# Attention on one core: two thirds of a pair's scores move between the products of the pair in front, and the halves of the outputs move behind the next pair's first softmax step

## What is computed

```python
q = (hn @ w_q).reshape(bsz, seq_len, N_KV_HEADS, GQ, HEAD_DIM)
...
s = jnp.einsum('bnqkgd,bnskd->bnkgqs', q, k) * (HEAD_DIM ** -0.5)
s = s + bias[None]                       # ALiBi, banded by chunks of 64 frames
sk = sink[None, None, :, :, None, None]
m = jnp.maximum(jnp.max(s, axis=-1, keepdims=True), sk)
p = jnp.exp(s - m)
p = p / (jnp.sum(p, axis=-1, keepdims=True) + jnp.exp(sk - m))
o = jnp.einsum('bnkgqs,bnskd->bnqkgd', p, v)
...
return jnp.concatenate([o_meta, o_real], axis=1) @ w_o
```

## Time and profile before

| what | us |
|---|---|
| three runs, median (lowest to highest) | 1196.5 (1194.91 to 1196.95) |
| the profiled execution: its own time | 1193.38 |
| span of its records | 1191.6 |
| TensorE busy in the span | 1114.3 (94%) |
| VectorE, ScalarE, GpSimd busy | 495.5, 486.4, 639.2 |
| stretch 651 to 757 of the span (the eight pairs): TensorE busy | 94.26 of 106.00 |
| mean granted TensorE clock | 0.969 |

### The profile page before, as it was taken

How to read it: one execution, slowest core, us unless ns; L and a number is a source line. 1 busy time by engine, 2 the same in 40 slices (tenths; PEclk the granted TensorE clock), 3 DMA queues, 4 the chain that set the end, 5 groups by cost and what they waited for, 6 DMA issues and landing times.

```text
span 1191.6 us, 28327 instructions
## 1 busy us (share of the span) xinstructions
PE 1114.3 (94%) x10546; PEld 1091.9 (92%) x10546; DVE 495.5 (42%) x853; ACT 486.4 (41%) x880; POOL 639.2 (54%) x540
## 2 busy tenths in 40 slices
PE   4576899999999999999999989899999999999996
PEld 3465799999999999999999888899999999999996
DVE  6988121254444444311115766435444444421111
ACT  5843243444444444322324544445444444432222
POOL 4993065555555555664544454665555555565451
PEclk7589899999999999999999999999999999999998
DMA  7055533333333333332323333233333333333321
GB/s 151 17 138 136 144 107 89 88 87 91 88 88 88 88 88 93 106 98 87 94 71 84 99 82 82 72 88 90 96 89 96 88 88 97 98 109 87 96 62 71
DMA packets 218326, 110.51 MB, mean 93 GB/s; under 512 B 33207, under 2 KB 215367, under 8 KB 217943
## 3 DMA queue, kind: packets, MB, share of 16 engines
q1 hardware_dynamic: 212327, 105.68, 31.9%
q10 hardware_dynamic: 5938, 3.99, 1.1%
HBM read 103.31 MB, written 6.32 MB: 92 GB/s over the span
## 4 chain that ended last, share of the span: by engine, by line
PE 82%; DVE 4%; DMA 3%; issue 3%; ACT 3%; POOL 2%; SPq 1%; ACTq 1%; POOLq 0%; DVEq 0%
PE slot L1199 77%; DMA brow<-in_s_b_im 1%; POOL w_lo L1916 1%; PE slot L1120 1%; POOL prob L2030 1%; PE slot L1114 1%; DMA xt<-in_x 1%; PE slot L1083 1%; ACT prob L961 1%; PE slot L1067 1%; PE slot L1097 0%; DMA v_scratch<-vtok 0%; ACT x_raw L736 0%; DMA kern_scratch<-kern 0%; ACTq L463 0%
## 5 line engine op out<-in xcount | busy, mean ns | idle before, releaser
L1916 POOL TENSOR_TENSOR w_lo<-raw,w_hi 128x512 fp32r<-128x512 f32 (+2 forms) x312 | 430.0, 1381 | 433.5 <-ACT w_hi L624 418.4
L624 ACT ACTIVATE w_hi<-raw 128x512 fp32r<-128x512 f32 (+2 forms) x308 | 202.5, 662 | 395.8 <-PE slot L1199 392.0
L1199 PE MATMUL slot<-xa_hi,w_hi 128*128 128x264 f32 (+1 forms) x1472 | 298.6, 284 | 0.9 <-DVE xa_lo L1678 0.9
L1199 PE MATMUL slot<-xa_hi,w_lo 128*128 128x264 f32 (+1 forms) x1472 | 298.4, 284 | 0.0
L1199 PE MATMUL slot<-xa_lo,w_hi 128*128 128x264 f32 (+1 forms) x1472 | 298.1, 284 | 0.0
L1199 PEld LDWEIGHTS slot<-xa_hi,w_hi 128*128 128x128 f32 x1472 | 229.0, 189 | 1.3 <-issue 1.1
L1199 PEld LDWEIGHTS slot<-xa_lo,w_hi 128*128 128x128 f32 x1472 | 228.3, 189 | 0.0
L1199 PEld LDWEIGHTS slot<-xa_hi,w_lo 128*128 128x128 f32 x1472 | 227.8, 189 | 0.0
L1199 PE MATMUL slot<-act_hi,w_hi 128*128 128x264 f32 (+1 forms) x704 | 141.8, 282 | 0.0
L1199 PE MATMUL slot<-act_lo,w_hi 128*128 128x264 f32 (+1 forms) x704 | 141.6, 282 | 0.0
L1199 PE MATMUL slot<-act_hi,w_lo 128*128 128x264 f32 (+1 forms) x704 | 141.2, 282 | 0.0
(11 more groups left out here) (285 smaller groups left out, 1481.0 us busy)
## 6 DMA issues: line engine op xcount, KB each, us to landing
raw<-in_ffn_w_up SPq DMA_DIRECT2D x176, 256.0 KB, 2.9
raw<-in_ffn_w_down SPq DMA_DIRECT2D x32, 384.0 KB, 3.3
raw<-in_ffn_w_down SPq DMA_DIRECT2D x32, 320.0 KB, 3.0
raw<-in_s_w_glu SPq DMA_DIRECT2D x32, 256.0 KB, 2.8
toep<-kern_scratch SPq DMA_DIRECT2D x64, 64.0 KB, 2.6
raw<-in_w_q SPq DMA_DIRECT2D x16, 256.0 KB, 3.3
raw<-in_w_o SPq DMA_DIRECT2D x16, 256.0 KB, 2.8
gelu_scratch<-x_raw ACTq DMA_DIRECT2D x8, 264.0 KB, 2.5
```

Of the source, the lines that this page charges most:

```text
L624: run(buffer_of(w_hi_all, buf, nk), buffer_of(raw_all, buf, nk), ACT.Copy).then_inc(hi_done, 1)
L1199: ins = mm(slot[dst][:, half, 0:b - a], w, xx[:, k, a:b], start=k == 0 and n == 0, stop=k == nk - 1 and n == 2)
L1916: tt(buffer_of(w_lo_all, buf, nk), buffer_of(raw_all, buf, nk), f32(buffer_of(w_hi_all, buf, nk)), ALU.subtract).then_inc(lo_done, 1)
```

## The change

Three pieces of work are put at other places; none is added or removed.

- TensorE: the scores of a pair's groups 0 and 1 (`first_scores`, 12 of 18 matmuls) are issued in the pair in front of it, behind that pair's product of group 0, and those of group 2 (`last_scores`) behind its product of group 2. The waits for the queries (`q_evicted`), for K (`k_in`) and for the copies out of the banks of groups 0 and 1 stand before the third block of the product of group 0; the first two stood before the product of group 2.
- ScalarE: the high half of a pair's output (`high_half`) is copied in the next pair, behind the exponentials of its group 0.
- VectorE: the low half (`low_half`) is written in the next pair, behind `scores(2)`, before the denominators of group 1.

In the last pair, the slab of the output projection no longer waits at its start for all seven outputs, but before each k tile for that one (`out_ready`).

The two halves that belong to the last pair stand behind it, as before.

```diff
@@ -950,6 +950,11 @@
                     slot[2][:, :, :].rearrange("p a (n c) -> p a n c", n=4), ACT.Copy).then_inc(v_copied, 1)
                 run(vtok[0:META, 4, :], slot[3][0:META, 0, 0:2 * P], ACT.Copy).then_inc(v_copied, 1)
 
+                def high_half(hp):
+                    act.wait_ge(pv_done, hp + 1)
+                    run(tile_of(ao_hi, hp, META, L), slot[2][:, 1, :], ACT.Copy)
+                    run(tile_of(ao_hi, hp, 0, META), slot[3][:, 0, 0:META], ACT.Copy).then_inc(ao_hi_done, 1)
+
                 def heads(j, hp, par):
 
                     for t in range(GRP):
@@ -961,11 +966,14 @@
                             ins = run(prob[:, par, n, :], prob[:, par, n, :], ACT.Exp, bias=mneg[:, par, n:n + 1],
                                       accum_out=den[:, par, n:n + 1])
                         ins.then_inc(exp_done, 1)
+                        if t == 0:
+
+                            if not isinstance(hp, int):
+                                high_half(act.snap(hp - 1))
+                            elif hp >= 1:
+                                high_half(hp - 1)
                     for n in range(2):
                         split_at(S_Q, j, 4 + 2 * par + n, KC)
-                    act.wait_ge(pv_done, hp + 1)
-                    run(tile_of(ao_hi, hp, META, L), slot[2][:, 1, :], ACT.Copy)
-                    run(tile_of(ao_hi, hp, 0, META), slot[3][:, 0, 0:META], ACT.Copy).then_inc(ao_hi_done, 1)
 
                 heads(0, 0, 0)
                 heads(0, 1, 1)
@@ -974,6 +982,7 @@
                         heads(j, act.snap(j * 2 + e), e)
                 heads(KVH - 1, HP - 2, 0)
                 heads(KVH - 1, HP - 1, 1)
+                high_half(HP - 1)
 
 
                 def o_tile(j, m, par):
@@ -1332,30 +1341,35 @@
                 bank = [slot[1][:, 0, :], slot[1][:, 1, :], slot[2][:, 0, :]]
                 o_real, o_meta = slot[2][:, 1, :], slot[3][:, 0, :]
 
+                def score(e, t, n):
+                    for x in range(2):
+                        part, rows = (slice(h * CH, (h + 1) * CH) for h in (x, x ^ SWAP[t]))
+                        ins = mm(bank[t][rows, n * KEYS:(n + 1) * KEYS], qt[part, e, GRP * t + n, :],
+                                 kcur[part, GRP * t + n, :], start=True, stop=True)
+                    if n == GRP - 1:
+                        ins.then_inc(scores_done, 1)
+
+                def first_scores(e):
+
+                    for n in range(GRP):
+                        score(e, 0, n)
+                        score(e, 1, n)
+
+                def last_scores(e):
+                    for n in range(GRP):
+                        score(e, 2, n)
+
+                def out_ready(k):
+                    pe.wait_ge(ao_hi_done, k + 1)
+                    pe.wait_ge(ao_lo_done, k + 1)
+
                 def heads(j, hp, e, ahead):
                     peeled = isinstance(hp, int)
-                    def score(t, n):
-                        for x in range(2):
-                            part, rows = (slice(h * CH, (h + 1) * CH) for h in (x, x ^ SWAP[t]))
-                            ins = mm(bank[t][rows, n * KEYS:(n + 1) * KEYS], qt[part, e, GRP * t + n, :],
-                                     kcur[part, GRP * t + n, :], start=True, stop=True)
-                        if n == GRP - 1:
-                            ins.then_inc(scores_done, 1)
-
-
-                    for n in range(GRP):
-                        score(0, n)
-                        score(1, n)
-                    for n in range(GRP):
-                        score(2, n)
                     if ahead:
                         q_slab(hp + 1, 1 - e, part=(0, Q_PART))
-
                     else:
                         pe.wait_ge(q_evicted, HP)
-                        pe.wait_ge(ao_hi_done, HP - 1)
-                        pe.wait_ge(ao_lo_done, HP - 1)
-                        slab(S_O, (KC, KC), 0, 0, ao_hi, ao_lo, tokens=LIVE_TOKENS, part=(0, HP - 1))
+                        slab(S_O, (KC, KC), 0, 0, ao_hi, ao_lo, ready=out_ready, tokens=LIVE_TOKENS, part=(0, HP - 1))
 
                     def transposes(t):
                         pe.wait_ge(p_ready, hp * GRP + (t + 1))
@@ -1364,11 +1378,18 @@
                         tr(bank[t][0:GRP * META, GRP * P:(GRP + 1) * P], probm[:, e, GRP * t:GRP * (t + 1), :].rearrange("p n j -> p (n j)"),
                            ident[:, :]).then_inc(pt_full, 1)
 
-                    def product(t):
+                    def product(t, scores_next=False):
 
                         pe.wait_ge(pt_copied, hp * GRP + (t + 1))
                         for n in range(GRP):
                             blk = GRP * t + n
+                            if scores_next and n == GRP - 1:
+
+
+                                pe.wait_ge(q_evicted, hp + 2)
+                                if e == 1:
+                                    pe.wait_ge(k_in, j * 96 + 192)
+                                pe.wait_ge(pt_copied, hp * GRP + 2)
                             for half in range(2):
                                 part = slice(half * HD, (half + 1) * HD)
                                 src = slice((half ^ SWAP[t]) * HD, ((half ^ SWAP[t]) + 1) * HD)
@@ -1387,17 +1408,18 @@
                     if not peeled or hp >= 1:
                         pe.wait_ge(ao_lo_done, hp)
                     pe.wait_ge(v_in, j * 80 + 80)
-                    product(0)
+                    product(0, ahead)
+                    if ahead:
+                        first_scores(1 - e)
                     product(1)
+                    product(2).then_inc(pv_done, 1)
                     if ahead:
-                        pe.wait_ge(q_evicted, hp + 2)
-                        if e == 1:
-                            pe.wait_ge(k_in, j * 96 + 192)
-
-                    product(2).then_inc(pv_done, 1)
+                        last_scores(1 - e)
 
                 pe.wait_ge(q_evicted, 1)
                 pe.wait_ge(k_in, 96)
+                first_scores(0)
+                last_scores(0)
                 heads(0, 0, 0, True)
                 heads(0, 1, 1, True)
                 with pe.Fori(1, KVH - 1) as j:
@@ -1781,6 +1803,11 @@
                     scores(1)
                     denominators(0)
                     scores(2)
+
+                    if not isinstance(hp, int):
+                        low_half(dve.snap(hp - 1))
+                    elif hp >= 1:
+                        low_half(hp - 1)
                     denominators(1)
                     denominators(2)
                     for t in range(GRP):
@@ -1793,6 +1820,7 @@
                         copy(pt[:, three, :], bank[t][:, 0:GRP * P].rearrange("p (n q) -> p n q", n=GRP))
                         copy(ptm[0:GRP * META, t, :], bank[t][0:GRP * META, GRP * P:(GRP + 1) * P]
                              ).then_inc(pt_copied, 1)
+                def low_half(hp):
                     dve.wait_ge(ao_hi_done, hp + 1)
                     tt(tile_of(ao_lo, hp, META, L), slot[2][:, 1, :], f32(tile_of(ao_hi, hp, META, L)), ALU.subtract)
                     tt(tile_of(ao_lo, hp, 0, META), slot[3][:, 0, 0:META], f32(tile_of(ao_hi, hp, 0, META)), ALU.subtract
@@ -1810,6 +1838,7 @@
                 chain.leave(KVH - 2, per)
                 heads(HP - 2, 0, True)
                 heads(HP - 1, 1, False)
+                low_half(HP - 1)
                 loop_2(KD, lambda m, e: update("o", m, e, G_FFN[1], m * 2 + (S_O + 2)))
 
             up_x_low(KD - 1)
```

## The result

Five executions of the changed kernel took 1184.62 us in the median (1183.09 to 1184.95), five of the kernel before beside them 1195.55 (1191.17 to 1196.95): a ratio of 0.9909, interval 0.989 to 0.9927, so 8.7 to 13.1 us faster.

A forecast was written before the change was run, and what follows sets the result against it. TensorE was taken to bound the kernel, with 11.7 us of waits removable; less 2.8, 1.2 and 0.2 this saves 7.5. The profiled execution would become 1185.9, plus 3.1 to the runs' median: 1189.0 us, range 1185 to 1192.5.

The forecast's parts named there:

- What bounds the kernel, and the ceiling of 11.7: TensorE sets the pace; its 14 waits for GpSimd's probabilities in pairs 1 to 7, 11.7 us, are the most to gain.
- The chain after the change: Scores to probabilities: VectorE starts at P+2.10, P being the products' first load; group 1 and 2 waits go, 0.55 and 0.49 spare.
- The chain stays in part: Rival: a chain 0.55 longer brings back group 1's wait; 0.3 left in each of seven pairs, 1191 us, chance 0.15.
- Output halves "covered": Moving the halves costs VectorE and ScalarE nothing, covered by the 5 us query slab; without margins 0.7 each.
- Two more changes between kinds: TensorE, pairs 0 to 6: extra products-to-scores and scores-to-products steps cost 0.40 a pair, 2.8 us in all.
- The new steps are free: Rival: neither the changes between kinds nor the queries' wait show; 11.7 less 0.2 saved, 1185 us, chance 0.12.
- The queries must be there earlier: TensorE waits for the queries at the product's third block, 0.2 us in pairs 1 to 6: 1.2 in all.
- The short idle that was to show it: Expected sign: short idle of the weight loads at the product's third block, released by VectorE's `qt`.
- Pair 7, and the small rest: No slab piece lies between pair 7's last two transposes, so about 0.2 of its 1.28 us wait stays.
- K late: Rival: K for the next head lands too late for the third block in pairs 1, 3, 5; 1199 or more, chance 0.04.

The follow-up runs named there:

- more_seams: Changed kernel with group 2's six scores spread between the blocks of the last product, four more steps between kinds per pair: 1189.79 us, 0.9955 of the kernel before.
- halves_late: Changed kernel with both output halves moved behind the last exponentials and last denominators: 82.42 us from pair 0's to pair 7's products against 80.67; not timed.
- c_before: The kernel before, unchanged, measured again: 1192.6 us, ratio 0.9991.
- c_after: The changed kernel, unedited, measured again: 1186.09 us, 0.9926 of the kernel before.
- halves_only: Changed kernel with all 18 score matmuls back behind the products, only the output halves moved: 1188.55 us, 0.9957 of the kernel before.
- best: Changed kernel with the three waits before the third block's very last matmul and all 18 scores behind the first product: 1186.0 us, 0.9926 of the kernel before.
- after: The changed kernel itself, as first measured against the kernel before: 1184.62 us, ratio 0.9909.
- waits_later: Changed kernel with its three waits moved before the third block's second half, the queries' last: 1185.57 us, 0.9928 of the kernel before.
- waits_behind: Changed kernel with its three waits before the third block's very last matmul, the queries' last: 79.64 us from pair 0's to pair 7's products against 80.67; not timed.

## Why the prediction was right, and where it failed

**What bounds the kernel, and the ceiling of 11.7.** Right. Of the waits at the transposes 11.66 us went, and TensorE's pace took the gain over unchanged: 8.4 ahead at the end of the attention and at the end of the program.

**The chain after the change.** Right to a tenth: VectorE at P+2.14 (P+2.10 forecast), low half at P+7.19 (P+7.10), period 11.58 (11.6), and the waits at group 1 and group 2 both gone. The margins are 0.40 and 0.43 in place of 0.55 and 0.49, so the rival "The chain stays in part" was not far off.

**Output halves "covered".** Right at the place where they stand, with less freedom than the text suggests: 1.7 us dearer in the late place, and without moving them the scores' part is a loss of 7.1. The forecast worked out the two edits in one sum and didn't see that one of them alone has the other sign.

**Two more changes between kinds.** 0.40 a pair was forecast. Measured are 0.36 by the starts of loads (0.15 + 0.21) and 0.30 by more_seams: 2.1 to 2.5 in place of 2.8. The rival "The new steps are free" falls with more_seams.

**The queries must be there earlier.** The place and the releaser are right, VectorE's two copies and the `qt` pieces. 0.2 was forecast, 0.13 came in six pairs and 0.19 more in two of them, where K's count is worked out behind the wait for the queries: 1.16 in place of 1.2. The sum agrees partly by luck, since that computation was not in the forecast and 0.13 alone would have given 0.8. The short idle that was to show it stands in no bracket of the profile after, only in the start of the third block; in halves_late, where it is longer, the bracket names VectorE's `qt`, as forecast.

**Pair 7, and the small rest.** 0.2 was put down for pair 7; its wait is all but gone, 0.06 is left of the transposes' waits beyond those of pair 0. Some 0.3 goes into the slab-to-products part, 7.29 against 7.24 worked out without waits. With the steps at 0.36 the account closes: 11.66 removed, less 2.5, 1.16 and 0.3, is 7.7. With 0.30 it gives 8.1, so the terms are known to some 0.4 and not better.

**K late.** Didn't occur. The landing took 2.4 to 3.1 us as before:

```profile
DMA to landing us min/median/max: 2.4/2.8/3.1
```

**The step that failed** is the last of the sum: "It is 3.1 below the median of the runs; I take the difference from the median: 1189.0." The stage's gain was forecast at 7.5 and measured at 7.7. But the three runs had their median at the upper end of what this kernel shows: single executions of it lay between 1189.37 and 1197.68 afterwards, its medians in the four comparisons were 1195.55, 1194.79, 1194.61 and 1193.76, and the median of all 52 executions is 1194.5. From the profiled execution's own 1193.38 the same 7.5 gives 1185.9; the changed kernel's medians were 1184.62, 1186.09 and 1185.59. The range had the same fault. It was built from the costs in the attention alone, and had no room for the spread of the two medians, 2 to 3 us: even the whole ceiling of 11.7, taken from 1196.5, ends at 1184.8, above the measured 1184.62. c_before and c_after show that this spread is no property of the change.

The distance from 1189.0 to 1184.62 is 4.4 us. Of it 0.9 is the base (1196.5 against 1195.55 beside the changed kernel), 0.2 the stage, and 3.2 is what this one comparison shows beyond the stage's 7.7.

What stays open is why these 3.2 fell to one side: the first ratio, 0.9909, lies with its whole interval beyond the 0.9936 that 7.7 us would be; the two later ones (0.9926, 0.9932) include it. I take it for the same spread with few executions. For it speaks that the medians of other comparisons miss the stage's figure to both sides: halves_only 6.2 against 3.1, the kernel before against itself 2.2 against 0.2 in its seven periods, best 7.8 against 9.8. No run shows the cause in the first comparison itself. Nor is it settled what sets the clock on one course or the other in the first 160 us.

## What to carry to other kernels

When work is moved forward on the engine that sets the pace, look at what the next engine does in front of it: early scores are worth nothing, and cost 7 us, as long as that engine first waits for something that the move has made later. The small costs count: the steps between kinds of tile, 0.15 to 0.21 us each, and a count worked out behind a late wait, 0.19 us, took a fifth to a quarter of what the removed waits gave. And measure a stage by the distance between two of its instructions in the trace, which repeated here to 0.2 us, not by the difference of two whole times, which did not to 3.

## What the runs showed of the hardware

- **A change between kinds of tile on TensorE** costs time of its own, without a semaphore: 0.15 us from 128*64 to 64*64 tiles, 0.21 from 64*64 to 128*64 or to the full array, by the starts of loads in after at a granted clock of 1.00; four of them in a pair cost 0.60 in more_seams, 0.12 less than these add up to.
- **A register computation behind a late wait** is paid in full: in after, pairs 3 and 5, working out K's count and reading the two semaphores behind it puts the load 0.22 us behind the queries in place of 0.06, and 0.19 into the period (11.77 against 11.58). Ahead of the late wait it cost nothing (waits_later, 11.56 and 11.57). The order in which waits take effect is not always that of the source: it has to be read from the trace.
- **Holding one of two tiles that run beside each other** gains next to nothing (waits_later, 11.57 against 11.58); holding only the last accumulating matmul gains 0.13 (waits_behind, 11.45).
- **The same code took between 660.9 and 666.6 us** to the start of the products, in 13 profiles, and the first 130 us, where the granted clocks differ most, are a stretch in which TensorE is busy six tenths of the time and its clock is granted at 0.69 to 0.78. From near 200 us to the products the 13 profiles agree within 0.3 us.
